# Fetching the tokens of a turn's slots as rows by indirect DMA, in place of products with pick columns, in a two-layer trunk with a grouped mixture of experts

## The chip, the cores and the metric

The kernel runs on one core of one Trainium2 chip. The metric is the device time of one execution in microseconds (us). Before the change three runs gave 1049.21, 1050.37 and 1052.34 us; the median is 1050.37 us.

## The reference, cut to what matters

256 latent tokens of 1024 channels pass two layers. Each layer has a mixer (attention and short convolution in the first, a Conformer convolution in the second) and then a mixture of 16 experts in 4 groups of 4. Each token goes to one group, and there to two experts. The part that matters here:

```python
def route(t, router_w, router_b):
    scores = jax.nn.sigmoid((t @ router_w).astype(jnp.float32))
    sel = (scores + router_b).reshape(n, N_GROUPS, EXPERTS_PER_GROUP)
    g_star = jnp.argmax(jnp.sum(lax.top_k(sel, TOP_K)[0], axis=-1), axis=-1)
    _, loc = lax.top_k(in_grp, TOP_K)          # in_grp: the scores of group g_star
    w = w / jnp.sum(w, axis=-1, keepdims=True)
    ...
for e in range(N_EXPERTS):
    y = (jax.nn.silu(t @ w1[e]) * (t @ w3[e])) @ w2[e]
    out = out + gates[:, e:e + 1] * y
```

All in float32, with w1 and w3 of 1024 x 512 and w2 of 512 x 1024 for each expert and layer: 201 MB of expert weights in all, each read once.

## The kernel before, in words

**Turns.** Tokens are sorted into tiles of 128 slots. In a turn one tile of slots meets the four experts of one group. The first layer (L = 0) has four turns, one for each group. The second (L = 1) has three such turns, for the three groups with fewer tokens, and then `wide(0)`, where each of the four experts of the largest group has a tile of its own with only the tokens that chose it. All turns but the last of a layer run in a hardware loop (`Fori`).

**Units.** A turn is 48 units of weights (`W_GROUP`), each 128 x 1024 float32 (512 KB). SP loads unit j into a ring of 8 (`raw`), ACT rounds it into the high half (`whi`, ring of 6, L712), DVE forms the low half (`wlo = raw - whi`, L1326), and PE makes six products of 128x128 by 128x512 with the unit (`three`, L1674 to L1676): high by high, low by high, high by low. A `raw` slot is free for the next load once DVE has formed `wlo`, a `whi` slot once PE has used it. ACT and DVE so run up to six units ahead of PE.

**Gather.** The stationary operand of the w1 and w3 products is `xghi`/`xglo`: the tile's tokens with channels on partitions, split in two halves. It comes from PE: `gather` (L1910) multiplies `htok` (tokens on partitions) by the columns of `pick`, a matrix with a 1 where a token sits in a slot. This takes 8 blocks of 128 channels times 2 halves of the tokens, 16 float32 products of 128x128 by 128x128, each of which is two records in the trace. ACT copies the result from PSUM into `xghi` (L880), DVE forms `xglo` (L1349). The gather for tile g+1 stands in turn g at unit 44, right behind the transposes of the last expert's hidden values (`transpose_hidden`, L1979, 4 transposes), whose result ACT (`hidThi`, L864) and DVE (`hidTlo`, L1389) split before the w2 products of unit 44 may start. In `wide(0)` the tiles of experts 1, 2 and 3 are gathered by `wide_gather` (L2027) at units 4, 12 and 20; that of expert 0 is gathered in the turn before. Experts 1 and 3 use `xg2hi`/`xg2lo`.

**Order of the work.** Every engine has its own list of instructions, written out by hand. A line such as `if j == SCATTER[i] + 6` puts an extra piece of work in front of unit j on that engine. `scatter` (PE, at units 10, 13, 16, 19) brings a finished tile's result back to token order, and `x_add` (DVE, six units later in DVE's list) adds it to `xres`. PE's scatter i waits for DVE's x_add i-1, since they share a PSUM bank. POOL issues small DMAs and is otherwise idle in the expert turns.

**Routing.** Ahead of the first turn of a layer, DVE and PE compute which slot each token has; PE makes the per-slot gates (L1931) into PSUM and DVE reduces them (`gspill` L1526, `gturn` L1527). In the last looped turn of the second layer PE makes the gates of the wide tiles (`wide_gates`, L1945), which ACT copies at unit 3 of `wide(0)` (`gate_copy`, L834).

## Time and profile before

| what | value |
|---|---|
| median of three runs | 1050.37 us (1049.21 to 1052.34) |
| the profiled execution: its own time, its span | 1051.65 us, 1049.8 us |
| mean granted TensorE clock | 0.970 of full speed |
| busy share of the span: PE, DVE, ACT, POOL | 94%, 74%, 59%, 8% |
| moved by DMA | 300.92 MB, mean 287 GB/s |
| turns of the first layer | 252 to 551 us of the span |
| turns of the second layer, wide(0) the last | 719 to 1037 us |

The span runs from the first to the last instruction. PE's busy time counts each product from its start to its modelled end, and products overlap, so what a piece of work costs PE is read from the start of its first product to the start of the product behind it.

### The profile page before, as it was taken

To read this page: it belongs to the slowest core of one execution; us is meant where nothing else is said; L and a number is where in the kernel's file an instruction comes from. 1 tells how busy PE (TensorE), PEld (TensorE's weight loads), DVE (VectorE), ACT (ScalarE), POOL (GpSimd) and SP (SyncE) were. 2 spreads that over 40 slices of the span, in tenths; PEclk is the share of its full clock that TensorE was granted. 3 is DMA by queue.
4 is the path that set the end of the run, shared out by engine and by line. 5 is a ranking of instruction groups with operands and counts; after the bars stand their busy time and mean duration, and the time that the engine had idled before them with its cause. 6 is when DMAs were issued, how large, how long until landed. Compare 5 with 4: busy or idle time off the path is not lost.

```text
span 1049.8 us, 17000 instructions
## 1 busy us (share of the span) xinstructions
PE 982.2 (94%) x6124; PEld 781.3 (74%) x6124; DVE 776.0 (74%) x952; ACT 617.7 (59%) x763; POOL 86.9 (8%) x150
## 2 busy tenths in 40 slices
PE   3899999998999999999996999888999999999996
PEld 0479884587788888888874886677788888888884
DVE  1544268557998998989967533758988989979894
ACT  2533326425778778777755323427778777767682
POOL 4091000100000000000000632000000000000000
PEclk8799999997999999999998999988999999999998
DMA  9997859665999998998986874929998998987871
GB/s 336 342 247 234 284 192 315 220 212 193 369 364 307 355 350 311 348 362 307 350 314 214 252 201 157 367 75 339 365 367 301 350 362 304 362 295 252 286 264 42
DMA packets 143043, 300.92 MB, mean 287 GB/s; under 512 B 13462, under 2 KB 44326, under 8 KB 142963
## 3 DMA queue, kind: packets, MB, share of 16 engines
q1 hardware_dynamic: 135360, 286.53, 77.9%
q0 software_dynamic: 6080, 12.66, 4.2%
q10 hardware_dynamic: 1530, 0.78, 0.3%
q8 instruction: 44, 0.72, 0.3%
q14 instruction: 29, 0.23, 0.1%
HBM read 292.35 MB, written 2.92 MB: 281 GB/s over the span
## 4 chain that ended last, share of the span: by engine, by line
PE 82%; DVE 7%; issue 3%; DMA 3%; ACT 3%; ACTq 0%; DVEq 0%; SPq 0%
PE ps L1674 16%; PE ps L1676 16%; PE ps L1675 16%; PE ps L2160 3%; PE ps L1916 3%; PE ps L1776 2%; PE ps L1686 2%; PE ps L1778 2%; PE ps L1777 2%; PE ps L2185 2%; PE ps L2187 2%; PE ps L2186 2%; PE ps L1794 2%; PE ps L1796 1%; PE ps L1795 1%
## 5 line engine op out<-in xcount | busy, mean ns | idle before, releaser
L1326 DVE TENSOR_TENSOR wlo<-raw,whi 128x1024 fp32r<-128x1024 f32 x384 | 455.9, 1220 | 42.1 <-ACT whi L712 40.6
L712 ACT CAST whi<-raw 128x1024 fp32r<-128x1024 f32 x384 | 396.8, 1051 | 115.4 <-PE ps L1676 103.5
L1674 PE MATMUL ps<-whi,xghi 128*128 128x512 f32 x480 | 192.8, 402 | 1.0 <-DVE wlo L1326 0.8
L1676 PE MATMUL ps<-wlo,xghi 128*128 128x512 f32 x480 | 190.3, 396 | 0.0
L1675 PE MATMUL ps<-whi,xglo 128*128 128x512 f32 x480 | 190.1, 396 | 0.0
L1055 DVE TENSOR_TENSOR wlo<-raw,whi 128x1024 fp32r<-128x1024 f32 x56 | 75.0, 1378 | 57.3 <-ACT whi L707 57.3
L1674 PEld LDWEIGHTS ps<-whi,xghi 128*128 128x128 f32 x480 | 90.4, 188 | 24.1 <-DVE wlo L1326 3.1
L1676 PEld LDWEIGHTS ps<-wlo,xghi 128*128 128x128 f32 x480 | 90.3, 188 | 21.8
L1675 PEld LDWEIGHTS ps<-whi,xglo 128*128 128x128 f32 x480 | 90.6, 189 | 20.6
L1674 PE MATMUL ps<-whi,hidThi 128*128 128x512 f32 x256 | 102.4, 400 | 2.9 <-DVE hidTlo L1389 1.5
L1676 PE MATMUL ps<-wlo,hidThi 128*128 128x512 f32 x256 | 101.4, 396 | 0.0
L1675 PE MATMUL ps<-whi,hidTlo 128*128 128x512 f32 x256 | 101.4, 396 | 0.0
L707 ACT CAST whi<-raw 128x1024 fp32r<-128x1024 f32 x56 | 56.5, 1046 | 32.3 <-DMA raw<-in_na_w_in 9.6
L1686 PE MATMUL ps<-raw,pair 128*32 128x256 f32 x768 | 60.9, 425 | 13.6 <-DMA raw<-in_w_mod 10.5
L1674 PEld LDWEIGHTS ps<-whi,hidThi 128*128 128x128 f32 x256 | 48.2, 188 | 14.5 <-issue 3.4
L1676 PEld LDWEIGHTS ps<-wlo,hidThi 128*128 128x128 f32 x256 | 48.2, 188 | 11.8
L1675 PEld LDWEIGHTS ps<-whi,hidTlo 128*128 128x128 f32 x256 | 48.2, 188 | 11.2
L1776 PE MATMUL ps<-hThi,whi 128*128 128x256 f32 (+1 forms) x160 | 51.2, 320 | 4.0 <-DVE hTlo L1120 4.0
L1778 PE MATMUL ps<-hTlo,whi 128*128 128x256 f32 (+1 forms) x160 | 49.3, 308 | 0.0
L1777 PE MATMUL ps<-hThi,wlo 128*128 128x256 f32 (+1 forms) x160 | 49.0, 306 | 0.0
L1686 PEld LDWEIGHTS ps<-raw,pair 128*32 128x32 f32 x768 | 20.4, 116 | 37.5 <-DMA raw<-in_w_mod 15.6
L2185 PE MATMUL ps<-fThi,whi 128*128 128x256 f32 x128 | 38.0, 297 | 4.4 <-DVE fTlo L1598 4.4
(313 smaller groups left out, 1484.3 us busy)
## 6 DMA issues: line engine op xcount, KB each, us to landing
raw<-in_moe_w SPq DMA_DIRECT2D x384, 512.0 KB, 5.2
raw<-in_w_mod SPq DMA_DIRECT2D x96, 512.0 KB, 6.2
raw<-in_na_w_in SPq DMA_DIRECT2D x24, 512.0 KB, 8.5
raw<-in_cf_pw_w SPq DMA_DIRECT2D x24, 512.0 KB, 8.8
mods<-mod_scratch POOLq DMA_DIRECT2D x9, 512.0 KB, 6.8
raw<-in_ab_w_out SPq DMA_DIRECT2D x8, 512.0 KB, 4.9
urep<-uT SPq DMA_DIRECT2D x64, 35.5 KB, 2.9
urep<-uT POOLq DMA_DIRECT2D x64, 35.5 KB, 2.8
```

What stands on the lines that cost most here:

```text
L707: A.copy(whi[:, n % SPL, :], raw[:, u % RAW, :]).then_inc(w_rounded, 1)
L712: A.copy(whi[:, (MOE_W[tn.L] + j) % SPL, :], raw[:, (MOE_U[tn.L] + j) % RAW, :]).then_inc(tn.sem("w_rounded"), 1)
L1055: V.tensor_tensor(wlo[:, n % SPL, :], raw[:, u % RAW, :], whi[:, n % SPL, :], ALU.subtract).then_inc(unit_done, 1)
L1326: V.tensor_tensor(wlo[:, n % SPL, :], raw[:, (MOE_U[L] + j) % RAW, :], whi[:, n % SPL, :], ALU.subtract).then_inc(tn.sem("unit_done"), 1)
L1674: T.matmul(dst, lhi, rhi, start=first, stop=False)
L1675: T.matmul(dst, llo, rhi, start=False, stop=False)
L1676: return T.matmul(dst, lhi, rlo, start=False, stop=last)
L1686: ins = T.matmul(ps[q * QUAD:(q + 1) * QUAD, bank, 0:QW], pair[:, k, :], raw[:, u % RAW, q * QW:(q + 1) * QW], start=(k == 0), stop=(k == ...
L1776: T.matmul(dst, wpart(n0, k, 0, m * P, P), acts(k, 0), start=(k == 0), stop=False)
L1777: i2 = T.matmul(dst, wpart(n0, k, 1, m * P, P), acts(k, 0), start=False, stop=False)
L1778: i3 = T.matmul(dst, wpart(n0, k, 0, m * P, P), acts(k, 1), start=False, stop=(k == KC - 1))
L2185: T.matmul(dst, wpart2(done_n, k, 0, m * P, P), a0, start=(k == 0), stop=False)
```

## The change

The normalised tokens `htok` are written once in each layer to a scratch in DRAM (1 MB, `tok_scratch`). PE forms for each slot the number of the token in it: a product of the pick columns with a column of constants (`token_number`), one float32 column wide. DVE copies these numbers as integers to `places`. POOL issues, for each tile but the first, an indirect DMA that fetches the 128 rows of 4 KB that `places` names to `xrow` (512 KB, one buffer), once the tile before has been consumed. PE then makes 8 transposes of `xrow` in place of the 16 products. This holds for 8 of the 12 tiles: three in the first layer, two in the looped turns of the second, and those of experts 1, 2 and 3 in `wide(0)`. The first tile of each layer and the tile of expert 0 in `wide(0)` are gathered by products as before. The copy of the wide gates moves from ACT (unit 3 of `wide(0)`) to DVE (ahead of unit 0).

```diff
+            def tokens_out(L):
+                eng.wait_ge(h_set, 4 * L + 2)
+                eng.dma_start(tok_scratch[L].rearrange("(t p) d -> p t d", p=P), htok[:]).then_inc(tok_out[L], 16)
+                eng.wait_ge(tok_out[L], 16)
+            def fetch_rows(L, column):
+                eng.indirect_dma_start(xrow[:], None, tok_scratch[L], bass.IndirectOffsetOnAxis(ap=places[:, column:column + 1], axis=0)) \
+                   .then_inc(rows_of, 16)
...
             mod_next(7)
+            tokens_out(0)
+            eng.wait_ge(places_set, 1)
+            for tile in range(1, GROUPS):
+                if tile > 1:
+                    eng.wait_ge(gathered, tile)
+                fetch_rows(0, tile - 1)
...
             eng.dma_start(mods[:, 0:D], final_g.partition_broadcast(P)).then_inc(final_in, 16)
+            tokens_out(1)
+            eng.wait_ge(places_set, 2)
+            for tile in range(1, GROUPS - 1):
+                eng.wait_ge(gathered, GROUPS + tile)
+                fetch_rows(1, tile - 1)
+            eng.wait_ge(places_set, 3)
+            for e in range(1, PER_GROUP):
+                eng.wait_ge(gathered, 2 * GROUPS - 1 if e == 1 else 2 * GROUPS + e - 1)
+                fetch_rows(1, e - 1)
...
                     for j in range(W_GROUP):
-                        if j == 3 and i == 0:
-                            gate_copy(tn)
...
                     if i:
                         wide_pick(i)
                         wide_xg_rest(tn, i, 0)
+                    else:
+                        tn.wait(eng, "spread_T", 1)
+                        V.tensor_copy(gate_of[:], ps[:, BX, GATES:GATES + PER_GROUP]).then_inc(tn.sem("spread_set"), 1)
+                        V.tensor_copy(places[:, 0:PER_GROUP - 1], ps[:, BX, GATES + PER_GROUP + 1:GATES + 2 * PER_GROUP]) \
+                         .then_inc(places_set, 1)
...
                 eng.wait_ge(route_pe, 4 * L + 4)
+                V.tensor_copy(places[:, 0:LOOPS[L] - 1], ps[:, BX, PLACES:PLACES + LOOPS[L] - 1]).then_inc(places_set, 1)
...
+                token_number = lambda t: cst[:, C_TOK + t:C_TOK + t + 1]
+                for tile in range(1, LOOPS[L]):
+                    for t in range(NT):
+                        ins = T.matmul(ps[:, BX, PLACES + tile - 1:PLACES + tile], pick[:, t, tile * P:(tile + 1) * P],
+                                       token_number(t), start=(t == 0), stop=(t == NT - 1))
                 ins.then_inc(route_pe, 1)
+                def rows_turned(b):
+                    for k in range(KC):
+                        ins = T.transpose(ps[:, b + k // 4, (k % 4) * P:(k % 4 + 1) * P], xrow[:, k * P:(k + 1) * P], ident)
+                    return ins
...
+                    for e in range(1, PER_GROUP if i == 0 else 0):
+                        for t in range(NT):
+                            at_ = GATES + PER_GROUP + e
+                            ins = T.matmul(ps[:, BX, at_:at_ + 1], of(t, e), token_number(t),
                                            start=(t == 0), stop=(t == NT - 1))
...
                                 if looped and ee == PER_GROUP - 1 and ahead:
-                                    gather(tn.g + 1)
+                                    if prepare:
+                                        gather(tn.g + 1)
+                                    else:
+                                        eng.wait_ge(rows_of, tn.g * 16 + (48 * L + 16))
+                                        rows_turned(0).then_inc(gathered, 1)
...
-                def wide_gather(tn, e):
+                def wide_gather(tn, e, i):
+                    if i == 0:
+                        eng.wait_ge(rows_of, 16 * (5 + e))
+                        rows_turned(WIDE_XG[e]).then_inc(tn.sem("gathered"), 1)
+                        return
                     for k in range(KC):
...
```

On PE, at unit 44 of a looped turn of the first layer, before (`cst` is the identity, `hid` an expert's hidden values):

```order
L1676 MATMUL ps<-wlo,hidThi 128x512
L206 REGISTER_ALU
L1982 MATMUL ps<-cst,hid 128x128 x4
L1916 ISA
L1916 MATMUL ps<-pick,htok 128x128
L1916 ISA
L1916 MATMUL ps<-pick,htok 128x128 x15
L206 REGISTER_ALU
L1674 MATMUL ps<-whi,hidThi 128x512
```

The same place of PE's list after the change:

```order
L1715 MATMUL ps<-wlo,hidThi 128x512
L207 REGISTER_ALU
L2037 MATMUL ps<-cst,hid 128x128 x4
L2066 ISA
L1981 MATMUL ps<-cst,xrow 128x128 x8
L207 REGISTER_ALU
L1713 MATMUL ps<-whi,hidThi 128x512
```

Sixteen products became eight transposes of `xrow`; nothing else moved there, and the w2 products of unit 44 still follow.

On DVE, at the end of the last turn before `wide(0)` and the start of `wide(0)`, before (with what each waits for):

```order
L1326 TENSOR_TENSOR wlo<-raw,whi 128x1024 [waits w_rounded] x3
L1389 TENSOR_TENSOR hidTlo<-ps,hidThi 128x512 [waits hidT_rounded]
L1326 TENSOR_TENSOR wlo<-raw,whi 128x1024 [waits w_rounded] x2
L1349 TENSOR_TENSOR xglo<-ps,xghi 128x512 [waits xg_rounded] x2
L1326 TENSOR_TENSOR wlo<-raw,whi 128x1024 [waits w_rounded] x3
```

The same place of DVE's list after the change:

```order
L1359 TENSOR_TENSOR wlo<-raw,whi 128x1024 [waits w_rounded] x3
L1422 TENSOR_TENSOR hidTlo<-ps,hidThi 128x512 [waits hidT_rounded]
L1521 COPY gate_of<-ps 128x4 [waits spread_T]
L1522 CAST places<-ps 128x3
L1359 TENSOR_TENSOR wlo<-raw,whi 128x1024 [waits w_rounded] x2
L1382 TENSOR_TENSOR xglo<-ps,xghi 128x512 [waits xg_rounded] x2
```

The two small copies are new there; before, the `wlo` rows followed `hidTlo` directly.

On POOL, the end of its list before (`mods` are the modulation rows, `final_g` the gain of the last norm):

```order
L618 DMA mod_scratch<-mrow 4x256 [waits mod_row]
L624 DMA mods<-mod_scratch 128x1024 [waits mod_out0]
L618 DMA mod_scratch<-mrow 4x256 [waits mod_row]
L624 DMA mods<-mod_scratch 128x1024 [waits mod_out1]
L693 DMA mods<-in_final_g 128x1024 [waits h_set]
```

The end of POOL's list after the change:

```order
L718 DMA mods<-in_final_g 128x1024 [waits h_set]
L680 DMA tok_scratch<-htok 128x2x1024 [waits h_set]
L685 DMA xrow<-tok_scratch,places 128x1024 [waits gathered,places_set,tok_out1]
L685 DMA xrow<-tok_scratch,places 128x1024 [waits gathered]
L685 DMA xrow<-tok_scratch,places 128x1024 [waits gathered,places_set]
L685 DMA xrow<-tok_scratch,places 128x1024 [waits gathered] x2
```

Six DMAs stand behind the one of `final_g` that was the last.

## Rows read from the trace of the kernel before

**Rows 1.** The page: busy us, share of the span, instructions.
```profile
PE 982.2 (94%) x6124; PEld 781.3 (74%) x6124; DVE 776.0 (74%) x952; ACT 617.7 (59%) x763; POOL 86.9 (8%) x150
```

**Rows 2.** Windows: stretch, length, busy us of each engine, PE clock, DMA share, GB/s.
```profile
325.00:400.00 75.00, 75.00 (x347) 61.17 (x346) 67.88 (x67) 58.25 (x63) 0.00 (x0) 1.00 0.94 336
...
944.00:1037.00 93.00, 91.46 (x454) 75.50 (x453) 77.37 (x77) 60.76 (x69) 0.00 (x0) 1.00 0.66 226
```

**Rows 3.** Waits of ACT, 250 to 550 us: total us, times, longest.
```profile
ACT whi L712 <- PE ps L1676: 50.9, 123, 2.3
```

**Rows 4.** Timeline of PE, a looped turn at unit 44: start, length, [idle before].
```profile
394.36 0.60 PE L1982 MATMUL ps<-cst,hid 128*128 128x128 f32 x4
394.80 3.74 PE L1916 MATMUL ps<-pick,htok 128*128 x32
398.29 0.48 PE L1674 MATMUL ps<-whi,hidThi 128*128 128x512 f32 x1
```

**Rows 5.** Timeline, unit 44 of the first layer's last turn, without gather.
```profile
543.58 0.60 PE L1982 MATMUL ps<-cst,hid 128*128 128x128 f32 x4
...
545.67 0.47 PE L1674 MATMUL ps<-whi,hidThi 128*128 128x512 f32 x1 [1.49 <-DVE hidTlo L1389]
```

**Rows 6.** Timeline of PE in wide(0): the gathers of experts 1 and 2.
```profile
954.31 3.73 PE L2032 MATMUL ps<-pick,htok 128*128 128x128 f32 x32
957.80 0.48 PE L1674 MATMUL ps<-whi,xghi 128*128 128x512 f32 x1
...
970.01 3.74 PE L2032 MATMUL ps<-pick,htok 128*128 128x128 f32 x32
973.50 0.48 PE L1674 MATMUL ps<-whi,xg2hi 128*128 128x512 f32 x1
...
979.65 0.39 PE L1975 MATMUL ps<-yhi,spread 128*128 128x512 f32 x1
```

**Rows 7.** Timeline of PE: the products one column wide for the wide gates.
```profile
931.30 1.84 PE L1953 MATMUL ps<-wsel,pick 128*128 128x1 f32 x16
```

**Rows 8.** Timeline, start of the first layer's turns, DVE and PE.
```profile
252.37 0.17 DVE L1526 TENSOR_REDUCE gspill<-ps 128x4 f32<-128x16 f32 x1 [0.68 <-PE ps L1931]
...
273.82 0.50 PE L1975 MATMUL ps<-yhi,spread 128*128 128x512 f32 x1 [1.29 <-DVE xres L1367]
```

**Rows 9.** Timeline, start of the second layer's turns, DVE and ACT.
```profile
721.13 3.50 DVE L1326 TENSOR_TENSOR wlo<-raw,whi 128x1024 fp32r<-128x1024 f32 x3 [1.72 <-ACT whi L712]
735.79 1.05 ACT L712 CAST whi<-raw 128x1024 fp32r<-128x1024 f32 x1 [0.30 <-DMA raw<-in_moe_w]
```

**Rows 10.** Windows there, columns as in rows 2.
```profile
706.00:709.00 3.00, 1.27 (x6) 1.19 (x6) 1.41 (x8) 0.00 (x0) 0.00 (x0) 0.50 0.11 45
...
724.00:727.00 3.00, 2.93 (x14) 2.04 (x12) 3.00 (x4) 2.94 (x4) 0.00 (x0) 1.00 1.05 387
```

**Rows 11.** Timeline of DVE around and in wide(0).
```profile
939.96 0.69 DVE L1389 TENSOR_TENSOR hidTlo<-ps,hidThi 128x512 fp32r<-128x512 f32 x1 [1.50 <-ACT hidThi L864]
944.97 2.36 DVE L1326 TENSOR_TENSOR wlo<-raw,whi 128x1024 fp32r<-128x1024 f32 x2 [4.32 <-ACT whi L712]
...
958.70 1.29 DVE L1455 TENSOR_TENSOR xg2lo<-ps,xg2hi 128x512 fp32r<-128x512 f32 x2 [2.23 <-ACT xg2hi L907]
...
977.46 0.68 DVE L1367 TENSOR_TENSOR xres<-xres,ps 128x512 f32<-128x512 f32 x1
```

**Rows 12.** DMA issues of the page: queue, count, KB each, median us to landing.
```profile
mods<-mod_scratch POOLq DMA_DIRECT2D x9, 512.0 KB, 6.8
bias_scratch<-rpbt POOLq DMA_DIRECT2D x1, 1792.0 KB, 16.7
```

**Rows 13.** Instructions of POOL and DVE side by side, 73 to 85 us.
```profile
73.42 11.21 DVE L1055 TENSOR_TENSOR wlo<-raw,whi 128x1024 fp32r<-128x1024 f32 x2 [6.99 <-ACT whi L707]
...
73.70 8.70 POOL L654 TENSOR_TENSOR bias<-bias,cst 128x512 f32<-128x512 f32 x8
```

**Rows 14.** Line L1055: ns min/median/max of one.
```profile
L1055 DVE TENSOR_TENSOR wlo<-raw,whi x56: 1211/1219/10075, 38.9 to 678.1; 128x1024 fp32r<-128x1024 f32 x56
```

More of the change, by code:

```diff
@@ L58 @@
 C_STACK = C_OFF + PER_GROUP ** 2
-C_N = C_STACK + QUAD
+C_TOK = C_STACK + QUAD
+C_N = C_TOK + NT
 R_C, R_CC, R_G, R_B, R_CONV, R_PW1, R_DWB, R_LNG, R_LNB = 0, 8, 16, 24, 40, 52, 68, 76, 84
@@ L229, in program @@
             cf_pw1_w, cf_pw1_b, cf_dw_w, cf_dw_b, cf_ln_g, cf_ln_b, cf_pw2_w, cf_pw2_b, router_w, router_b,
-            moe_w1, moe_w3, moe_w2, final_g, consts, bias_scratch, mod_scratch, out):
+            moe_w1, moe_w3, moe_w2, final_g, consts, bias_scratch, mod_scratch, tok_scratch0, tok_scratch1, out):
     with ExitStack() as stack:
@@ L258, in program @@
         flag = sb("flag", [P, 8], I32)
+        places = sb("places", [P, GROUPS], I32)
         pair = sb("pair", [P, KC, QUAD])
@@ L324, in program @@
         hTr = at("hTr", [P, KC, SEQ], 60)
+        xrow = at("xrow", [P, D], 68)
         xg2hi = at("xg2hi", [P, KC, P], 60, F32R)
@@ L418, in program @@
         gathered = sem("gathered")
+        tok_out = [sem("tok_out0"), sem("tok_out1")]
+        places_set = sem("places_set")
+        rows_of = sem("rows_of")
         xg_rounded = sem("xg_rounded")
@@ L667, in mod_next @@
                 mod_fill(v, mods[:, (v - 6) * D:(v - 5) * D])
+            tok_scratch = (tok_scratch0, tok_scratch1)
+            def tokens_out(L):
[5 more added lines that the diff above has]
+                   .then_inc(rows_of, 16)
             eng.wait_ge(h_set, 2)
@@ L693, in _ @@
             eng.dma_start(mods[:, 0:D], final_g.partition_broadcast(P)).then_inc(final_in, 16)
+            tokens_out(1)
[7 more added lines that the diff above has]
+                fetch_rows(1, e - 1)
+            eng.wait_ge(rows_of, 16 * 8)
             eng.wait_ge(final_in, 16)
@@ L1953, in wide_gates @@
                             ins = T.matmul(ps[:, BX, GATES + e:GATES + e + 1], of(t, e), wsel[:, 1, t, e:e + 1],
+                                           start=(t == 0), stop=(t == NT - 1))
+                    for e in range(1, PER_GROUP if i == 0 else 0):
+                        for t in range(NT):
+                            at_ = GATES + PER_GROUP + e
+                            ins = T.matmul(ps[:, BX, at_:at_ + 1], of(t, e), token_number(t),
                                            start=(t == 0), stop=(t == NT - 1))
@@ L2056, in wide @@
                         wide_gates(i)
-                        wide_gather(tn, 0)
+                        wide_gather(tn, 0, i)
                     else:
@@ L2081, in wide @@
                             if ee and j == WIDE_GATHER[ee]:
-                                wide_gather(tn, ee)
+                                wide_gather(tn, ee, i)
                         if j == W_GROUP - 2:
@@ L2241 @@
 GATES = 16
+PLACES = 96
 WIDE_GATHER = [None, 4, 12, 20]
@@ L2298, in shape_constants @@
     i, j = np.divmod(np.arange(PER_GROUP ** 2), PER_GROUP)
+    k[:, C_TOK:C_TOK + NT] = np.arange(P)[:, None] + P * np.arange(NT)
     k[:, C_STACK:C_STACK + QUAD] = np.tile(np.eye(QUAD), (P // QUAD, 1))
@@ L2319 @@
     args.append(nc.dram_tensor("mod_scratch", [MODS, D], F32, kind="Internal").ap())
+    for L in range(2):
+        args.append(nc.dram_tensor(f"tok_scratch{L}", [SEQ, D], F32, kind="Internal").ap())
     args.append(nc.dram_tensor("out_0", [1, SEQ, D], F32, kind="ExternalOutput").ap())
```

## The prediction

> **What bounds the kernel now.** I read the page's engine shares first, then windows over the turns, then who waits, then timelines at each gather. PE is busy 94% of the span and DVE 74% [rows 1]. In a looped turn PE fills all of 75 us while DVE fills 67.9 and DMA 0.94 of its capacity [rows 2]. ACT waits for PE 123 times in the first layer's turns [rows 3]: the engines that feed PE stand ahead of it, stopped by the ring of six. Within a turn, a microsecond that leaves PE is therefore a microsecond of the kernel, as long as DVE (7 us of room per turn) and DMA (6% of 75 us, 4.5 us) keep up.
>
> **What the change removes.** A gather in a looped turn holds PE from 394.80 to 398.29, 3.49 us for 32 records, 0.109 us each [rows 4]. The four transposes ahead of it hold PE from 394.36 to 394.80, 0.44 us or 0.11 each [rows 4]. Eight transposes of `xrow` have the same form (128x128, stationary operand from SBUF, moving operand the identity or the data) and take 8 x 0.11 = 0.88 us. By that a gather alone becomes 2.6 us shorter.
>
> In a looped turn not all of this arrives. The w2 products behind the gather need `hidTlo`, which ACT and DVE make from the transposes ahead of it. The first layer's last turn has no gather and shows what this takes: 543.58 to 545.67, 2.09 us, of which PE idles 1.49 [rows 5]. With a gather the same stretch is 394.36 to 398.29, 3.93 us. After the change it needs the later of 0.44 + 0.88 = 1.32 us and 2.09 us. The hidden-value wait takes over, and each looped gather saves 3.93 - 2.09 = 1.84 us. Five of them: **9.2 us**.
>
> In `wide(0)` the products behind the gathers (units 4, 12, 20) don't need a fresh `hidTlo`, so each saves 2.6 us, 7.8 together [rows 6]. DVE must follow, and it has less room here. The `xg2lo` of expert 1 waits for the gather [rows 11], so DVE moves forward by 2.2 to 2.4 us with it, but from there it is busy without a stop until PE has saved twice 2.6. PE's scatter 2, at 979.65 [rows 6], needs the x_add of 977.46, which ends at 978.14 [rows 11]: 1.5 us of room. PE would come 5.2 us earlier, DVE 2.4 plus some tenths, so PE waits about 0.7 there. I take **7.1 us** for the three.
>
> **What it adds to PE.** Products one column wide: the wide gates are 16 records in 1.84 us [rows 7], which with the tail of the last one taken off is the 0.11 each of the gather's records, so one float32 product (two records) is 0.22 us. The numbers of the wide tiles are 3 x 2 products, **1.3 us**, in a stretch where PE has no gap: paid in full. The first layer has 3 x 2 ahead of its first turn, 1.3 us, and DVE's copy of `places` is 0.2. DVE waits there for PE's last routing product (0.68 us, [rows 8]) and is then busy without a gap until PE waits for its x_add at 273.82 (1.29 us, [rows 8]), so both lie on the path: **1.5 us**. In the second layer, 2 x 2 products (0.9 us) and the copy lie in a stretch in which DVE next waits 1.72 us for ACT's cast, which needs neither [rows 9]: nothing on DVE's path, and I put 0.3 for PE's own first units. DVE's two small copies ahead of `wide(0)` come behind `hidTlo` of 939.96, in 4.3 us in which DVE has nothing [rows 11]: nothing; the gates they wait for were done at 933.1 [rows 7].
>
> **What it adds to POOL and DMA.** Two writes of 1 MB and eight fetches of 0.52 MB, 6.3 MB. The write of the second layer is issued behind `final_g`, ahead of the expert loads, where DMA works at 0.11 of its capacity [rows 10]; it costs 0 to 1 us and I take 0. The second layer's first fetch falls in the only stretch where DMA is full, 387 GB/s at 1.05 [rows 10], and a cast waited 0.30 us for its load [rows 9]. It delays the loads by 0.52 MB / 387 GB/s = 1.4 us. DVE is busy 3.00 of 3.00 us there [rows 10] and so stands behind ACT, which hides it, I take it; without that cover it costs 1.4. A looped turn would carry 25.2 + 0.5 MB in about 73 us, 353 GB/s, under what DMA has shown.
>
> How long a fetch takes to land no row shows. The nearest: a DMA of the same 512 KB issued by POOL lands in 6.8 us; the DMA in the smallest pieces, 1792 KB, took 16.7 [rows 12]. I take 8 us. In the loops there are 70 us for it. In `wide(0)`: expert 1 from 941 (copy of `places`) to 954.31, 13.3 us; expert 2 from the end of one gather to the start of the next, 957.80 to 970.01, 12.2 us [rows 6]; expert 3, eight units later again, about 13. All three are covered at 8 us, none at 16.7.
>
> Each fetch also makes GpSimd read `places` from SBUF. What that can do to DVE is seen once: while POOL added the masks for 8.70 us, one `wlo` of DVE took 10.08 in place of 1.22 [rows 13, 14]. The Trainium skill (SBUF — State Buffer, "Who interferes with whom") says a DVE instruction with two SBUF inputs and a GpSimd instruction that reads SBUF exclude each other for a whole instruction. By that rule, the trace agrees. For an index read, the bounds are 0 and the 8.7 us of that row for each fetch; the reads are of 128 numbers, so I go near the low end and put **1.0 us** on the path for all eight.
>
> The Trainium skill (TensorE: Matmul & The Clock Gate, "Part 4: PE-mode transpose") gives 275 ns for a transpose of 128x128 in one kernel. The trace shows records of that length whose starts are 0.11 us apart [rows 4], so the rule is a latency here. Were it the pitch, eight would hold PE 2.2 us, a looped gather would save 1.3 and a wide one the same, and the sum would be 6 us; I give that 1 in 100.
>
> **Sum.** 9.2 + 7.1 - 1.3 - 1.5 - 0.3 - 1.0 = 12.2 us less. The profiled execution took 1051.65 us for its span of 1049.8; 12.2 less is 1039.4. The median of the runs lies 1.3 lower, so the forecast for the median is 1050.4 - 12.2 = **1038.2 us**. If DVE keeps up everywhere and nothing else is paid, it is 9.2 + 7.8 - 1.3 = 15.7 less, 1034.7.
>
> **Rivals.**
> (a) GpSimd's reads hold DVE up for longer. DVE has 0.4 to 1 us of room to PE's scatters once PE is faster. At 1.2 us a fetch (one `wlo`), some 0.6 us of each of the eight, or 5 us, reaches PE, and 4 of it beyond what I took: 1042.5. For it: rows 13; against it: POOL's other DMA issues beside `wlo` left no trace in its median of 1219 ns [rows 14].
> (b) Fetches land late in `wide(0)`, the case on the other side: slower than before. One GpSimd fetch names 128 separate rows, and many slots are empty and name the same row. The three covers sum to 38.5 us, so a landing time T above 13.3 costs 3T - 38.5: the gain is gone at T = 16.9, just above the 16.7 of rows 12. At 20 us it costs 21.5, and the time is 1059.7. Against it: 6.8 us for the same bytes.
> (c) DMA is already the bound and PE's idle shares hide it: then the shorter gather gives nothing back in the looped turns, and only the wide stage (DMA share 0.66, [rows 2]) gains, 7.1 - 1.3 - 1.5 - 0.3 - 1.0 = 3, less the 0.5 MB of each of five fetches, 1.4 x 5 = 7 at the full rate: if half of that is paid, no change, 1050. Against it: 0.94 with ACT waiting for PE and never, in those turns, for a load.
>
> **How the numbers follow.** The forecast with its near surroundings (1034.5 to 1041) 0.62; (a) 0.15, with the skill's transpose rule in it; (c) 0.08; (b) 0.11; some other loss of a few us, still faster, 0.04. The measurement can tell about 0.3%, 3.2 us. Faster by more: 0.62 + 0.15 + 0.04 + 0.02 of (c) = 0.83. Same: 0.06. Slower: 0.11. The range from 1034.5 (everything hidden, nothing else paid) to 1047 (a, and part of c) leaves out (b) and most of (c), a little under 2 in 10.
>
> **What would show it.** Right: timeline at a looped unit 44 with 8 transposes in under 1 us, an idle of 0.6 to 0.8 us on `hidTlo`, and 2.1 us for the stretch; in `wide(0)` gathers of 0.9 us with no idle ahead; turns of about 72.8 us; `xrow` landing in 5 to 10 us; DMA share about 0.97 in the looped turns. Wrong: PE idle on `xrow` (b), `wlo` records over 2 us near a fetch (a), ACT's casts waiting for `raw` in mid-turn (c), transposes of `xrow` 0.27 us apart.

## The result, and the profile after

The changed kernel takes 1034.42 us in the median of four runs (1031.83 to 1036.56), before 1050.92 beside it: ratio 0.9838, 95% interval 0.9821 to 0.9855. It is 16.5 us faster; the forecast was 12.2. In five further rounds it took 1034.84, ratio 0.985 [0.9829, 0.987]. The sign and the mechanism were right; the size was off by 4.3 us, and the time lies 0.1 us below the range that was forecast (1034.5 to 1047).

The profiled execution has a span of 1030.0 us. Its page, first line, answering to [rows 1]:

```profile
PE 960.6 (93%) x5964; PEld 761.7 (74%) x5964; DVE 775.1 (75%) x956; ACT 616.8 (60%) x762; POOL 97.0 (9%) x160
```

Windows of the changed kernel, columns as in [rows 2]. The second one is as far from the end of the span as the one of before; it starts 2.5 us ahead of unit 44 of the last looped turn, where that one started 5.3 us behind it:

```profile
325.00:400.00 75.00, 74.38 (x333) 60.23 (x332) 69.80 (x68) 60.22 (x65) 0.94 (x1) 1.00 0.98 355
924.00:1017.00 93.00, 90.74 (x431) 73.80 (x431) 78.09 (x80) 62.63 (x72) 3.58 (x3) 1.00 0.72 255
```

PE is no longer full in the first: it misses 0.62 us. The busy share of the DMA engines went from 0.94 to 0.98. The timeline of PE at unit 44 of a looped turn, answering to [rows 4], says what the 0.62 are:

```profile
390.66 0.60 PE L2037 MATMUL ps<-cst,hid 128*128 128x128 f32 x4
391.10 1.04 PE L1981 MATMUL ps<-cst,xrow 128*128 128x128 f32 x8
392.75 0.47 PE L1713 MATMUL ps<-whi,hidThi 128*128 128x512 f32 x1 [0.62 <-DVE hidTlo L1422]
```

From 390.66 to 392.75 it is 2.09 us, where it was 3.93: the eight transposes take the place of 3.49 us of products, and then PE waits 0.62 us for `hidTlo`. In `wide(0)` no such wait follows (timeline of PE, answering to [rows 6]); the third row is the wait for x_add at scatter 2:

```profile
955.01 1.04 PE L1981 MATMUL ps<-cst,xrow 128*128 128x128 f32 x8
955.80 0.47 PE L1713 MATMUL ps<-whi,xg2hi 128*128 128x512 f32 x1
...
962.77 0.50 PE L2030 MATMUL ps<-yhi,spread 128*128 128x512 f32 x1 [0.69 <-DVE xres L1400]
```

The tile `xrow`: its fetches on POOL (ns min/median/max) and their landing:

```profile
L685 POOL DMA_INDIRECT xrow<-tok_scratch,places x8: 944/962/1691, 252.2 to 956.6; - x8
...
DMA to landing us min/median/max: 4.2/6.3/7.5
```

No fetch came late: nothing on PE waited for `xrow`. One part of the trace speaks against the forecast. At unit 40 of the last looped turn the number products (L2008, `pick` times the column of token numbers in `cst`) stand behind the gates' (L2003; timeline of PE):

```profile
916.23 1.84 PE L2003 MATMUL ps<-wsel,pick 128*128 128x1 f32 x16
917.93 1.48 PE L2008 MATMUL ps<-cst,pick 128*128 128x1 f32 x12
919.27 0.48 PE L1713 MATMUL ps<-whi,hidThi 128*128 128x512 f32 x1
...
921.16 0.63 PE L1714 MATMUL ps<-whi,hidTlo 128*128 128x512 f32 x1
```

The 12 records take 1.34 us (917.93 to 919.27), as forecast, but from 920.75 on, 1.5 us after the last of them, eight products last 0.6 in place of 0.39 us. The window there shows the granted clock at 0.50, its lower level of 1.2 GHz:

```profile
920.80:924.00 3.20, 3.20 (x9) 2.52 (x8) 1.23 (x1) 1.46 (x2) 0.00 (x0) 0.50 0.95 361
```

**Stages of PE.** The table gives stretches between landmarks of PE's timeline, in us of each profile. Numbers in it are differences of start times, so they are free of what an execution gained or lost elsewhere.

| stretch | before | f1 (before again) | after | e1 (after again) |
|---|---|---|---|---|
| first gather of layer 1 to its first hidden transposes | 27.28 | 26.61 | 27.83 | 28.40 |
| three looped periods of the first layer | 223.82 | 223.82 | 217.21 | 217.13 |
| unchanged work between the layers' turns | 153.15 | 153.82 | 151.05 | 152.68 |
| one looped period of the second layer | 74.61 | 74.60 | 72.47 | 72.41 |
| last looped turn, unit 32 to unit 44 | 19.08 | 19.08 | 21.90 | 21.92 |
| wide(0): unit 44 of the turn ahead to unit 12 | 30.87 | 30.87 | 28.09 | 28.05 |
| wide(0), units 12 to 20 | 16.62 | 16.62 | 14.82 | 14.85 |
| wide(0), units 20 to 32 | 21.29 | 21.29 | 18.54 | 18.48 |

A looped period (from unit 44 of one turn to unit 44 of the next) lost 2.20 us, not 1.84, and repeats to 0.03 us. The stretch of unchanged work does not repeat: over all profiles it is 151 to 156 us, and the 2 us by which the first profile of after is short there are no gain of the change.

### The profile page after: what moved, and what is told of

It is laid out like the page before. It is cut to its first block, busy times and chain, and to the rows that moved or that the text cites. A ratio compares the mean times of both kernels' runs of the same rounds, so it can differ in the third digit from the quotient of the medians.

```text
span 1030.0 us, 16691 instructions
## 1 busy us (share of the span) xinstructions
PE 960.6 (93%) x5964; PEld 761.7 (74%) x5964; DVE 775.1 (75%) x956; ACT 616.8 (60%) x762; POOL 97.0 (9%) x160
## 3 DMA queue, kind: packets, MB, share of 16 engines
q0 software_dynamic: 7776, 18.96, 6.0%
## 4 chain that ended last, share of the span: by engine, by line
PE 81%; DVE 10%; DMA 3%; issue 3%; ACT 2%; SPq 0%; ACTq 0%; DVEq 0%
PE ps L1713 16%; PE ps L1715 16%; PE ps L1714 16%; DVE wlo L1359 3%; PE ps L2223 3%; PE ps L1815 2%; PE ps L1725 2%; PE ps L1817 2%; PE ps L1816 2%; PE ps L1833 2%; PE ps L2248 2%; PE ps L2250 2%; PE ps L2249 2%; PE ps L1835 1%; PE ps L1834 1%
## 5 line engine op out<-in xcount | busy, mean ns | idle before, releaser
L1714 PEld LDWEIGHTS ps<-whi,xglo 128*128 128x128 f32 x480 | 90.8, 189 | 20.4
L1713 PEld LDWEIGHTS ps<-whi,hidThi 128*128 128x128 f32 x256 | 48.5, 189 | 18.6 <-issue 7.5
L1714 PEld LDWEIGHTS ps<-whi,hidTlo 128*128 128x128 f32 x256 | 48.6, 190 | 11.1
L685 POOL DMA_INDIRECT xrow<-tok_scratch,places x8 | 8.5, 1061 | 410.8 <-PE ps L1981 229.6
```

Source lines behind the costliest of these rows:

```text
L1713: T.matmul(dst, lhi, rhi, start=first, stop=False)
L1714: T.matmul(dst, llo, rhi, start=False, stop=False)
```

## The experiments

Each was timed in five rounds against before on the same chip. Not all were on one chip, and the median of before lay between 1050.9 and 1052.2 us beside them; so a difference between the medians of two experiments is good to a us or two, and the one worked out from their ratios is given with it where the two differ. "Period" is one looped period of the first layer. The recorded expectations name their theories with letters; the text below keeps them.

**The parts one by one: e1 to e4.** e1 is the changed kernel itself.

> The changed kernel once more, for a narrower interval and a second profile. Theory A (three small costs of the forecast are not paid: number products at the layers' starts 1.8 us, index reads 1.0 us; the gains are as forecast): 9.2 + 7.1 - 1.3 = 15.0 us less than before, ratio 0.9857. Theory B (the forecast's sum is right and the first four runs were lucky): 12.2 us less, ratio 0.9884. Theory C (some gain that no term names, of 2 us or more): 17 us less or more, ratio 0.984 or below. In the profile, A and B expect the same pitch of products in unchanged code as before (0.2344 us), C may show another.

e2 keeps only the numbers:

```diff
-                                        rows_turned(0).then_inc(gathered, 1)
+                                    gather(tn.g + 1)
...
-                fetch_rows(0, tile - 1)
```

> The changed kernel with all tiles gathered by products, as before; nothing is written to DRAM or fetched. The products that form token numbers, DVE's copies of them and the moved gate copy stay. What is left is the price of the numbers alone. The forecast's terms: 1.5 + 0.3 + 1.3 = 3.1 us slower than before. Theory A: only those ahead of wide(0) are paid, 1.3 us slower; the first wait of PE at a scatter of the first layer stays near 1.3 us after a start moved by 1.5 by the forecast, and is not moved by A.

e3 keeps the looped rows and gives `wide_gather` its products back, without its numbers; e4 keeps those of `wide(0)` and has `gather` in the loops, without numbers at the layers' starts. Ahead of the `...` is the cut of e3, behind it that of e4:

```diff
                 def wide_gather(tn, e, i):
-                    if i == 0:
-                        eng.wait_ge(rows_of, 16 * (5 + e))
-                        rows_turned(WIDE_XG[e]).then_inc(tn.sem("gathered"), 1)
-                        return
...
-                                        rows_turned(0).then_inc(gathered, 1)
+                                    gather(tn.g + 1)
```

> Rows are fetched and transposed only in the looped turns (5 of the 8); wide(0) is gathered by products and its number products are left out. The forecast's terms: 9.2 - 1.5 - 0.3 - 0.6 (five of the eight index reads) = 6.8 us less than before. Theory A: 9.2 less, nothing else paid. Theory C: over 10.5 less; then the extra gain lies in the looped turns.

> Rows are fetched and transposed only in wide(0) (3 of the 8); the looped turns gather by products and the number products at the layers' starts are left out. The forecast's terms: 7.1 - 1.3 - 0.4 = 5.4 us less than before. Theory A: 5.8 less. Theory C: over 7 less; then the extra gain lies in wide(0). Together e3_looped_rows and e4_wide_rows should add up to the changed kernel's gain.

| kernel | median us | ratio [95%] | period | unit 32 to 44 |
|---|---|---|---|---|
| e1 | 1034.84 | 0.985 [0.9829, 0.987] | 72.38 | 21.92 |
| e2 | 1051.67 | 0.9998 [0.9987, 1.0009] | 74.25 | 21.89 |
| e3 | 1039.72 | 0.9889 [0.9871, 0.9907] | 72.41 | 19.00 |
| e4 | 1042.68 | 0.9918 [0.9899, 0.9937] | 74.25 | 21.89 |

e3 and e4 gain 11.7 and 8.6 us, 20.3 together, where the whole gains 15.8; each has the cost of its own numbers in it and not that of the other's, so the parts should add up. Something is counted twice, and it is in both. It shows in the periods of e2 and e4, which gather by products exactly as before and take 74.25 in place of 74.60 us. Theory A (only three costs were too high) fell: e2 should have been 1.3 slower and was level, though by its interval (0.9987 to 1.0009) only just; the comparison with f2 below is the stronger one. Theory C asked where the extra gain lies: not in the rows at all.

**What all changed kernels share: f1, f2, h1.** Their common part is storage: two columns more in `cst` (8 bytes), and `places` (16 bytes), which move all tiles behind them. These are the small tensors and the arena, one large tensor that holds `xghi`, `xglo`, `hidThi`, `hidTlo`, `pick`, `htok` and others; `raw`, `whi`, `wlo` and `xres` lie ahead and stay. So PE's stationary operands move, and its moving operands in these products do not.

> The kernel before, unchanged, for a second profile. In the first profile of before a product of 128x128 by 128x512 has a median of 397 ns and a looped turn takes 74.60 us; in the profile of the changed kernel and in those of e1 to e4 the median is 393 ns, and where a looped turn still gathers by products (e2, e4) it takes 74.25. Theory D (it is the chip or the execution): 397 and 74.60 are not tied to the kernel, and this profile may show 393 and 74.25. Theory E (it is tied to what all changed kernels share, the few added bytes in SBUF that move what lies behind them): 397 ns and 74.60 us again. The time is that of before, ratio 1.000, either way.

```diff
-C_N = C_STACK + QUAD
+C_TOK = C_STACK + QUAD
+C_N = C_TOK + NT
...
+        places = sb("places", [P, GROUPS], I32)
```

> The kernel before, with only the two added columns of constants and the small tensor of places allocated, and never used; every instruction stays. Theory E (moved addresses set PE's pace): 393 ns, a looped turn of 74.25 us, and 6 turns with wide(0) about 0.35 each less, 2.5 us in all, ratio 0.9976. Theory D: 397 and 393 ns as the chip has it, the same in f1 and f2 if they agree with each other, ratio 1.000.

f1: 1050.28, ratio 0.999 [0.9979, 1.0001]. f2: 1047.58, ratio 0.9962 [0.9949, 0.9974]. The products by line, of f1 and then of f2 (ns min/median/max):

```profile
L1674 PE MATMUL ps<-whi,xghi x480: 391/397/499, 250.3 to 999.3; 128*128 128x512 f32 x160
```

```profile
L1676 PE MATMUL ps<-whi,xghi x480: 390/393/505, 251.0 to 998.2; 128*128 128x512 f32 x160
```

397 and 393 ns, periods of 74.61 and 74.25. Not one instruction differs. h1 then moves the arena alone, by 32 bytes:

```diff
-        arena = nc.sbuf_base + 31 & ~31
+        arena = nc.sbuf_base + 63 & ~63
```

> f2 (two columns of constants and the tensor of places allocated, no instruction changed) was 3.6 us faster than before, with looped turns of 74.25 in place of 74.60 us. Those 24 bytes move the base of the arena (the tiles xghi, xglo, hidThi, hidTlo, pick, htok and others lie in it) from byte 154336 of a partition, 32 above a multiple of 64, to 154368, a multiple of 64; they also move the small tensors behind the constants. This kernel is before with nothing but the arena's base rounded up to a multiple of 64; constants and small tensors stay. Theory E1 (the alignment of the arena's tiles to 64 bytes sets PE's pace): products of 393 ns, looped turns of 74.25 us, about 1047.5 us, ratio 0.9962. Theory E2 (the small tensors or something else of the layout): 397 ns and 74.60, ratio 1.000.

1045.94, ratio 0.9956 [0.994, 0.9972], products 393 ns, period 74.25. E1 is shown so far as this: moving the arena of before from byte 154336 to 154368, a multiple of 64, gives 4 to 5 us, and a gain of this kind is in the changed kernel's without being its doing. The traces place 2.4 us of it in f2 and 2.6 in h1, from a layer's first hidden transposes to its last, both layers together; the rest of the 4 to 5 us is not located, and the intervals (2.7 to 5.4 us in f2, 2.9 to 6.3 in h1) reach down to nearly that. It is also what hid the numbers' price: e2 against f2 is 0.9998 / 0.9962 = 1.0036, 3.8 us, near the forecast's 3.1 (good to some 2 us; the stretches of PE add up to 5.4, see the table at the end).

**Which addresses: h2, j1, k1.** h2 and j1 put the arena of the changed kernel 32 and 96 bytes further on, k1 that of before 32 past the multiple:

```diff
-        arena = nc.sbuf_base + 31 & ~31
+        arena = (nc.sbuf_base + 63 & ~63) + 32
```

> The changed kernel with the arena's base put at 32 above a multiple of 64, as it was before. Theory E1: looped turns go from 72.40 to 72.75 us and the products from 393 to 397 ns; 3 to 3.6 us are lost, and 1038 us is what the change itself brings, which is the forecast. Theory E2: 1034.8 as e1, turns of 72.40.

> The changed kernel with the arena's base at byte 154464, which is 96 above a multiple of 128, as that of before was (154336); h2 had it at 154400, 32 above a multiple of 128. Theory E3 (the place within 128 bytes decides, and 96 is worse than 32): looped turns of 72.75 us, as many as 0.36 above e1, and about 1038 us. Theory E1 in its plain form (anything off a multiple of 64 is the same, and before's 0.36 came in part from the small tensors too): 72.53 as in h2, 1036.5.

> The kernel before with its arena at byte 154400 (32 above a multiple of 64, as 154336 is, and 64 bytes further on), nothing else moved. If every place off a multiple of 64 costs the kernel before the same: looped turns of 74.60 us, ratio 1.000. If the small tensors, which lie elsewhere in the changed kernel, have no part and 154336 is a worse place than 154400: 74.37 us (74.25 and the 0.12 of h2), ratio about 0.997.

| kernel | arena at | period | median us | ratio [95%] |
|---|---|---|---|---|
| before, f1 | 154336 | 74.61 | 1050.28 (f1) | 0.999 [0.9979, 1.0001] |
| k1 | 154400 | 74.39 | 1049.33 | 0.9978 [0.9969, 0.9988] |
| h1 | 154368 | 74.25 | 1045.94 | 0.9956 [0.994, 0.9972] |
| e1 | 154368 | 72.38 | 1034.84 | 0.985 [0.9829, 0.987] |
| h2 | 154400 | 72.54 | 1036.97 | 0.9866 [0.9839, 0.9893] |
| j1 | 154464 | 72.52 | 1034.68 | 0.9842 [0.9826, 0.9858] |

On the multiple the profiles of the changed kernel and its variants have periods of 72.38 to 72.41. Off it a period costs 0.11 to 0.16 us more in both kernels (k1, h2, j1), and 0.36 at the place that before happened to have. E3 fell: 154464 stands as 154336 does within 128 bytes, and costs 0.11 to 0.14. Nor do all products suffer alike. The three kinds of w1 and w3 products have medians of 397 ns each in before and of 393 each in h1, but in k1 (by line, ns min/median/max):

```profile
L1674 PE MATMUL ps<-whi,xghi x480: 389/399/503, 250.1 to 999.1; 128*128 128x512 f32 x160
...
L1675 PE MATMUL ps<-whi,xglo x480: 388/392/403, 250.4 to 999.4; 128*128 128x512 f32 x160
...
L1676 PE MATMUL ps<-wlo,xghi x480: 388/394/402, 250.6 to 999.6; 128*128 128x512 f32 x160
```

So "on or off a multiple of 64" is a summary of the places tried, not the mechanism. What makes 154336 worse than the other two is open; moving the changed kernel there needs its small tensors moved back too, and that wasn't tried. h2 and j1 differ by less than their intervals.

**Fetches and index reads: e5, f4.**

```diff
-            for tile in range(1, GROUPS):
+            for tile in range(1, 2):
```

> The changed kernel with two of the eight fetches left (the first of each layer); the other tiles transpose whatever rows lie in xrow, so their products are those of other tokens. All transposes stay. What is left out is six fetches of 0.5 MB and six index reads. The forecast's term of 1.0 us for eight index reads: 0.75 us faster than e1 (1034.8). Theory A (reads and fetches cost nothing while they land in time): the same as e1. A rival, that DMA traffic is on the path: up to 6 x 1.4 = 8 us faster.

```diff
+                for again in range(times):
                     eng.indirect_dma_start(xrow[:], None, tok_scratch[L], ...).then_inc(rows_of, 16)
+                    fetched[0] += 16
+                    if again < times - 1:
+                        eng.wait_ge(rows_of, fetched[0])
```

> The changed kernel with each of the five fetches of the looped turns made four times, one after the other; those of wide(0) once. 15 more fetches, index reads and 7.9 MB more. A turn has 70 us for them, and four at 6.3 us take 25. The forecast's term (1.0 / 8 us each): 1.9 us slower than e1. Theory A: the same as e1. The forecast's rival of GpSimd's reads (0.6 us on the path each): 9 us slower. If DMA were the bound (1.4 us each): 21 us slower.

e5 took 1035.13 us, ratio 0.9855 [0.9837, 0.9872]; f4 1035.72, ratio 0.9849 [0.9836, 0.9862]; e1 1034.84. Six fetches fewer or fifteen more: no difference. The times alone could not tell the 1.9 us of the forecast's term, but the periods can: three more fetches a turn would add 0.38 us to each, and f4 has 72.41 where the others have 72.38 to 72.41. In `wide(0)` e5, without its fetches, has the three stretches of e1 to 0.01 us. In f4 a window in mid-turn and the landing read:

```profile
325.00:400.00 75.00, 74.38 (x333) 60.21 (x332) 69.06 (x68) 60.22 (x65) 9.74 (x4) 1.00 1.00 372
```

```profile
L688 POOL DMA_INDIRECT xrow<-tok_scratch,places x23: 947/1122/6086, 253.8 to 962.8; - x23
...
DMA to landing us min/median/max: 4.0/7.8/13.0
```

The DMA engines are busy all the time, landings stretch to 13 us, and PE's busy time in the window is 74.38 us as in the changed kernel, the period 72.41. The forecast's rivals (a) and (c) are both refuted here. The median of `wlo` is the same 1218 ns, by line on DVE:

```profile
L1365 DVE TENSOR_TENSOR wlo<-raw,whi x384: 1206/1218/1228, 245.0 to 1011.0; 128x1024 fp32r<-128x1024 f32 x192
```

The rule of exclusion that the forecast took from the Trainium skill (SBUF — State Buffer, "Who interferes with whom") is not seen on the index read of an indirect DMA: 23 of them, and no `wlo` over 1228 ns, where [rows 14] has one of 10075 beside POOL's additions.

**A late fetch: g4.** g4 has the same loop of repeated fetches, three times for each tile of `wide(0)` and once elsewhere.

> The changed kernel with each of the three fetches of wide(0) made three times, one after the other, so that the rows stand ready only when the third has landed; the looped turns as in e1. This is the forecast's rival (b) brought about: covers of 12.2 to 13.3 us, cost 3T - 38.5 for a time T to the last landing. In the first fetch of a turn the single ones landed in 6.3 us and one issue takes 1 us of GpSimd, so three take about 20 us: 21.5 us slower than e1, 1056, slower than before. If DMA, less busy in wide(0), lands each in 4.5 us, T is 16 and the cost is 9.5: 1044. In both, PE idles on xrow at units 4, 12 and 20 by T less the cover. A rival, that other waits overlap with it and the cost is under half of 3T - 38.5: below 1040.

1059.04 us, ratio 1.0073 [1.0058, 1.0088]: 24.2 above e1 (23.4 by the ratios), slower than before. Timeline of PE, the three places, and what stands behind the second:

```profile
952.05 1.73 PE L1987 MATMUL ps<-cst,xrow 128*128 128x128 f32 x8 [4.34 <-DMA xrow<-tok_scratch,places]
...
974.52 1.97 PE L1987 MATMUL ps<-cst,xrow 128*128 128x128 f32 x8 [7.72 <-DMA xrow<-tok_scratch,places]
976.15 0.78 PE L1719 MATMUL ps<-whi,xg2hi 128*128 128x512 f32 x1
976.72 0.63 PE L1720 MATMUL ps<-whi,xg2lo 128*128 128x512 f32 x1
...
995.93 1.97 PE L1987 MATMUL ps<-cst,xrow 128*128 128x128 f32 x8 [4.95 <-DMA xrow<-tok_scratch,places]
```

The idle times sum to 17.0 us. From issue to use the three took 17.7, 20.5 and 18.9 us, by the forecast's form 57.1 - 38.5 = 18.6. But the three stretches of `wide(0)` grew by 6.2, 9.3 and 7.1, 22.6 together: behind each idle time products run at 0.63 us, at a granted clock of 0.50 (windows 954.00:955.70, 976.50:979.50 and 998.00:1000.00). So the form was near for the wait (18.6 against 17.0 us of idle time) and 4 us short of the whole, which also has what the lower clock takes. Rival (b) was real, and the change stays clear of it by landing in 6.3 us in place of 13.

**The number products and the clock: i1, e9.** In i1 `wsel` has a third plane with the tokens' numbers, written by one more DVE copy in the routing.

```diff
-                            ins = T.matmul(ps[:, BX, GATES + e:GATES + e + 1], of(t, e), wsel[:, 1, t, e:e + 1],
+                            ins = T.matmul(both[:, :, e], of(t, e), wsel[:, 1:3, t, e], start=(t == 0), stop=(t == NT - 1))
...
-                    for e in range(1, PER_GROUP if i == 0 else 0):
```

> The changed kernel with the numbers of the wide tiles made in the same eight products as the gates (the moving operand has two columns, the weight and the token's number), so the six extra products at unit 40 of the last looped turn are gone; DVE copies the numbers beside the weights once. In the profiles of the changed kernel the stretch from hid transposes at unit 32 to those at unit 44 takes 21.9 us with the extra products and 19.0 without: 1.34 are the products, and about 1.5 come behind them, where the granted clock is at its lower level for some 3.4 us (records of 0.63 in place of 0.39). Theory F (the longer run of one-column products brings the clock down): without the six the stretch takes 19.0, and the kernel gains 2.9 us, 1032.0. Theory G (the clock falls by itself, whatever stands there): 20.5, a gain of 1.3 us, 1033.5.

1031.91 us, ratio 0.9826 [0.981, 0.9843], 2.9 below e1 (2.5 by the ratios). The stretch from unit 32 to 44 is 19.00. The gate products carry the numbers at no cost (timeline of PE of i1):

```profile
918.98 1.84 PE L2005 MATMUL ps<-wsel,pick 128*128 128x2 f32 x16
```

In the nine profiles without the six extra products this stretch is 18.96 to 19.08, always. In the eleven with them it is 20.3 to 20.4 three times (e5, g4, j1), where no product is slow; 21.9 six times, where the clock falls at or shortly after the last of the twelve; and 23.5 twice (f4, e9), where it falls among the twelve, which then take 2.2 us and not 1.34. Timeline of PE of f4:

```profile
922.83 2.34 PE L2014 MATMUL ps<-cst,pick 128*128 128x1 f32 x12
925.03 0.77 PE L1719 MATMUL ps<-whi,hidThi 128*128 128x512 f32 x1
```

So F holds, though not in every execution. The Trainium skill (TensorE: Matmul & The Clock Gate, "Part 1: The HAM clock gate") says that the clock follows how busy the array has been; by that rule a longer run of products one column wide can bring it down, and these traces agree. e9 takes it further, at the layers' starts:

```diff
-                for tile in range(1, LOOPS[L]):
+                for tile in 4 * tuple(range(1, LOOPS[L])):
```

> The changed kernel with the number products at the layers' starts made four times over (18 more float32 products, 36 records, in the first layer; 12 products, 24 records, in the second), same results. The forecast took 1.3 + 0.2 us for them in the first layer as paid in full, and 0.3 of 0.9 in the second. Forecast: 3 x 1.3 + 0 to 3 x 0.9, so 3.9 to 6.6 us slower than e1. Theory H (a run of one-column products this long also brings the lower clock, 1.5 us for each episode): 2 to 3 us more than that, with records of 0.63 at the head of the first turns.

1047.1 us, 12.3 above e1 (10.8 by the ratios), beyond all that was expected. Timeline of PE of e9:

```profile
249.65 7.67 PE L1974 MATMUL ps<-cst,pick 128*128 128x1 f32 x48
257.19 0.77 PE L1713 MATMUL ps<-whi,xghi 128*128 128x512 f32 x1
257.76 0.63 PE L1714 MATMUL ps<-whi,xglo 128*128 128x512 f32 x1
```

48 records take 7.54 us, 0.157 each and not 0.11, and then the turn starts on the lower clock. Windows show when it fell, columns as in [rows 2]; in the second the records are 0.20 us apart:

```profile
249.70:252.60 2.90, 2.90 (x28) 2.90 (x28) 0.00 (x0) 2.89 (x4) 0.00 (x0) 1.00 0.05 19
252.70:257.10 4.40, 4.40 (x22) 4.40 (x22) 0.00 (x0) 1.10 (x2) 0.00 (x0) 0.50 0.00 0
```

Gather to first hidden transposes is 35.89 us against 28.40 in e1, the same in the second layer 30.25 against 26.38: 11.4 of the 12.3.

**The wait for hidTlo: e7, e8, i2.** e7 puts the four products that need only `hidThi` first at unit 44:

```diff
+                            if late:
+                                tn.wait(eng, "hidT_rounded", e + 1)
+                                for half in range(2):
+                                    T.matmul(ps[:, BY + half, :], hidThi[:, q, :], moe_slot(whi, n)[:, cut], ...)
+                                    T.matmul(ps[:, BY + half, :], hidThi[:, q, :], moe_slot(wlo, n)[:, cut], ...)
...
+                                if late:
+                                    ins = T.matmul(ps[:, BY + half, :], hidTlo[:, q, :], moe_slot(whi, n)[:, cut], ...)
```

> The changed kernel with the six products of each turn's unit 44, first block, in another order: the four that need only hidThi stand first, and the two with hidTlo behind them, so that PE waits only for ACT's hidThi there. In e1 a looped stretch of rows is 0.44 + 0.88 us of transposes and 0.62 of idle time for hidTlo; ACT's hidThi is done 1.25 us after the first transpose, when PE has just finished the rows. Theory (the wait for hidTlo is all that holds a looped gather to 1.84 us of gain): 5 x 0.62, and 2 x 0.75 at the two ends without a gather, 4.6 us less than e1, 1030.2. Rival (DVE or the ring of six is as late, and the idle time shows up behind the products): under 1.5 us less.

1030.43 us, ratio 0.9798 [0.9786, 0.9811], 4.4 below e1 (5.5 by the ratios) where 4.6 was expected; the stretches give 4.7 (five periods 0.65 shorter, and 0.73 at each of the two ends without a gather). Timeline of PE of e7:

```profile
391.89 1.04 PE L1981 MATMUL ps<-cst,xrow 128*128 128x128 f32 x8
392.82 0.47 PE L2075 MATMUL ps<-whi,hidThi 128*128 128x512 f32 x1
393.13 0.40 PE L2076 MATMUL ps<-wlo,hidThi 128*128 128x512 f32 x1
```

No idle time is left, and the period goes from 72.38 to 71.73. A looped gather now gains 2.5 us, nearly the 2.6 that the shorter piece gives by itself.

> The kernel before with the order of e7 (the four products with hidThi alone first). In before the 3.49 us of gather products cover the wait for hidTlo, so only the two places without a gather gain: 2 x 0.75 = 1.5 us less, ratio 0.9986, looped turns of 74.60 as before. Rival (the order is worth something by itself in every turn, 4.4 us as on the changed kernel): 1046.5, ratio 0.996, turns of 74.0.

e8: 1050.48 us, ratio 0.9984 [0.9973, 0.9996], period 74.61, the end of `wide(0)` 0.73 shorter. In before the gather covers that wait, as expected; the order pays only once the gather is short. i2 joins i1 and e7:

> The changed kernel with both: numbers joined to the gate products (i1, 1031.9, ratio 0.9826) and the order of e7. If the two add: 2.9 + 4.6 = 7.5 us less than e1, 1027.3, ratio 0.978. If one eats the other: 1030 or more.

1027.48 us, ratio 0.9773 [0.976, 0.9786]: 7.4 below e1 (8.1 by the ratios), 23 below before, the fastest version here.

## Why the prediction was right and where it failed

| term | forecast | measured, and where |
|---|---|---|
| five looped gathers | -9.2 | -9.2: periods 74.25 (e2, e4) to 72.41, 1.84 each |
| three wide gathers | -7.1 | -7.2: 2.71 + 1.72 + 2.77, f2's stretches against e1's |
| wide numbers | +1.3 | +2.9 in 6 of 11 profiles (after and e1 among them), +4.5 in 2, +1.3 in 3 |
| start of the first layer | +1.5 | +1.5: gather to first hidden transposes, mean of 7 profiles without the products 26.73, of 12 with them 28.23 |
| start of the second layer | +0.3 | +1.0: the same, 25.79 and 26.75 |
| index reads | +1.0 | none seen (e5, f4) |
| tiles moved in SBUF | none | -3.6 (f2), -5.0 (h1); 2.4 and 2.6 of it located in the turns |

Without the last row the measured terms sum to 11.0 us less, with it to 14.6 or 16.0; e1 measured 15.8.

**Right.** Each gain came where it was worked out, and the two sums of gains as large, to 0.1 us. The hidden-value wait took over in the looped turns with 0.62 us, and DVE's x_add held PE at scatter 2 for 0.69 where 0.7 was forecast. The fetches landed in time. The change itself, against before with the same addresses, is e1 against f2 or h1: 0.985 / 0.9962 = 0.9888, 11.8 us, or 0.985 / 0.9956 = 0.9894, 11.1 us; with the intervals of both ratios either is good to some 2 to 3 us. The forecast had 12.2.

**Failed.** The step that failed is the sum's last: "the median of the runs lies 1.3 lower, so the forecast for the median is 1050.4 - 12.2". It takes for granted that instructions which the change does not touch keep their durations. The diff adds 24 bytes in front of the arena, and these took 0.36 us off a period of 288 products of 128x512, 1.2 ns from one's start to the next's (the records' median fell from 397 to 393 ns): 3.6 to 5 us in all by f2 and h1. No term and no rival held this. The range's lower end, 1034.5, stood for "everything hidden, nothing else paid" and so could not hold it either. Whether a median falls a tenth of a us below that end or above it (1034.42, then 1034.84) is chance; that it comes so near although the three costs of the numbers were paid is due to the missing term. Its cause within the chip stays open.

**Mis-sized, in part against each other.** The wide numbers (1.3, measured 2.9 mostly): their records cost what was forecast, but the lower clock behind them wasn't priced. The index reads (1.0, none seen). The second layer's start (0.3, measured 1.0): the products were taken as hidden by DVE's wait for ACT, and were paid in full. That these three errors come to 1.3 us together and not to more is luck. In rival (a) the time is a few tenths too high: eight times 0.6 less the 1.0 taken is 3.8, which gives 1042.0 and not 1042.5. That the covers are 12 to 13 us and a landing above them costs all of it was right (g4), short of the clock's part.

**Left open.** Why 154336 is the worst of the places tried, and by what path the address acts. What the granted clock does at a layer's start varies from one execution to the next. Records of 0.63 stand in the head of the first turn in 4 of the 12 profiles with the number products (e9 aside), in that of the second layer in 2 of them, and in none of the 7 without. The four do not have the longer stretches (27.8 to 28.0 us, the other eight 28.0 to 28.7): in them the higher clock came earlier, within the gather. This is in the means above, not explained.

## What to carry to other kernels

When a change adds or resizes any tensor, first run the old kernel with the new layout alone: here 24 bytes of storage made about a quarter of the measured gain. When a piece of PE's work gets shorter, the wait behind it takes over, and can often be filled by reordering products by what they need. Operands that ride along in a product already made were free here (two columns in place of one, 1.84 us either way), while extra one-column products cost their own time and may cost the clock.

## What the runs showed of the hardware that was not expected

- The place of the arena, and with it of PE's stationary tiles, within a partition's bytes changes PE's pace, the moving tiles staying where they are: periods of 74.61, 74.39 or 74.25 us for arenas at 154336, 154400 and 154368. The products of 128x128 by 128x512 have medians of 397 ns in the first, 393 in the last, and 392 to 399 by operand in the middle one (k1, w1 and w3 products).
- At 28 records one column wide the clock fell to its lower level (granted 0.50) in 8 of 11 profiles: in six at or shortly after the last of them, for some 3.4 us, 1.5 us lost (in after products of 0.6 us from 920.75 to 924.15); in two among the last twelve, 3.1 us lost. Behind 16 such records, or 16 of two columns, it fell in none of 9. In a run of 48 the first 26 or so took 0.11 us each and the rest 0.20.
- An indirect DMA of 128 rows of 4 KB cost GpSimd 0.96 us and landed in 4.2 to 7.5 us, no later than plain ones of 512 KB from the same queue [rows 12]; with the DMA engines busy all the time (share 1.00), in up to 13 us.
- PE's idle times of 4 to 8 us on `xrow`, 17.0 together, made their stretches 22.6 us longer, a third more; the granted clock was 0.50 behind each of them.
